# One inference step of a hybrid encoder: the same kernel with its SBUF tensors at other addresses

## The chip, the cores and the metric

The kernel runs on one core of a Trainium2 chip. The metric is the time of one execution on the device in microseconds (us), as the median of several runs. One of its executions was also taken with the profiler; the rows below come from it.

## What is computed

One layer for 1,024 prompt tokens and 8 x 16 sample tokens (1,152 tokens in all) of width 1,024, in float32:

```python
def layer_step(x, ...):
    hn = rms_norm(x, g_pre_mix)
    z, xbc, dt_raw, q, k, v = jnp.split(hn @ w_in, IN_SPLITS, axis=-1)      # 1024 -> 3080 columns
    ...                                    # group A: conv, SiLU, chunked state-space scan
    ...                                    # group B: rotary, differential attention over chunks
    mix = jnp.concatenate([y_ssd, y_att], axis=-1) @ w_out
    h = x + rms_norm(mix, g_post_mix)
    qx = (rms_norm(h, g_pre_x) @ wq_x).reshape(bsz, l, MEM_HEADS, MEM_HEAD_DIM)
    ...                                    # cross-attention, 4 heads of 256, 256 memory tokens
    h = h + rms_norm(ox @ wo_x, g_post_x)
    hn = rms_norm(h, g_pre_ffn)
    f = (jax.nn.silu(hn @ w_gate) * (hn @ w_up)) @ w_down                   # hidden width 2816
    h = h + rms_norm(f, g_post_ffn)
    return h, k, v, ssm_new, conv_new
```

The memory keys and values (256 tokens through wk_x and wv_x) are computed too.

## The kernel before

**Large products.** Each float32 operand is split in two float32r tensors, a high and a low half (names end in `_hi`/`_lo`, or in H/L). Helper `three` (L220 to L230) makes one product of three matmuls for each of 8 slices of the contraction: high x high (L225), high x low (L228), low x high (L229); in the trace the name in front is the operand that streams (moving), the one behind it is the one loaded into the array (stationary). A unit has 24 matmuls and fills one PSUM bank. There are three shapes: 256 columns stream (token-major products: the input projection, the two joins after `w_out` and `wo_x`, the memory products), 384 columns (the convolution part, `wq_x`, gate and up), and 512 columns (the down product of the feed-forward part).

**Weights.** All weights come as 130 items of [128, 1024] in order. SyncE loads an item into `w_raw` (2 buffers, L463), GpSimd makes `w_hi` (L522) and `w_lo` (L524) of it (4 buffers each), and TensorE gives a buffer back with the semaphore `w_used`.

**Stages, in order of time.** Norm and transposes of the tokens, and the input projection with the memory products between its units (to about 290 us); convolution part (to 390); the state-space scan (390 to 510); attention of the prompt and of the samples (510 to 780); join 1 and `wq_x` (780 to 1,000); cross-attention (1,000 to 1,140); join 2 (to 1,270); the feed-forward loop of 11 groups (to 2,085); the last norm, the sum and the stores.

**SBUF.** Tensors are given their places in the order in which they are declared, one behind the other, each start rounded up to 32 bytes. The first one of the kernel starts at byte 16,512 of a partition. Four large regions of 36,864 bytes each are shared over time by the tensors of an `overlay` call: the regions of H (also QL, KL, OL, the memory tensors), of NH (YT, MIX, QX, OH, Hback), of NL (V, E, H2, the hidden tensors, and others) and of XC (the staging tensors, KTt, QTt, YH, ACC). Behind them lies a fifth region of 16,640 bytes (gB0, xp, qkr, xs and others). All offsets inside these regions are fixed by the shapes; the token slices step by 512 bytes, a row of 1,152 tokens is 4,608 bytes, and a chunk of 384 tokens is 1,536 bytes, all multiples of 512.

Of the kernel before, what the change touches and what calls it, by code (L numbers as in the profile page):

```python
# [17 lines left out]
P = 128  # L18
# [42 lines left out]
S_N, S_Q, S_V, S_END = 0, 40, 76, 96  # L61
# [5 lines left out]
def build(nc, x_in, mem_in, wall, wdt, consts, vecs, gains, rows, kc, vc, h0, sconv, cmk, cmv,  # L67
          y_o, k_o, v_o, ssm_o, conv_o, mk_o, mv_o, zs_d, q_d, h_d):
    with ExitStack() as ctx:
        def sb(name, shape, dt=F32):  # L70
            return ctx.enter_context(nc.sbuf_tensor(name, shape, dt))
# [2 lines left out]
            return ctx.enter_context(nc.semaphore(name))  # L74


        raw = [sb(f"w_raw{i}", [P, WI]) for i in range(2)]
        whi = [sb(f"w_hi{i}", [P, WI], F32R) for i in range(4)]
        wlo = [sb(f"w_lo{i}", [P, WI], F32R) for i in range(4)]
        stat = sb("stat", [P, S_END])  # L80
        cst = sb("cst", [P, C_END])
        vec = sb("vec", [P, V_END])
        ones = sb("ones", [P, P])
# [2 lines left out]
        nlam = sb("nlam", [P, 1])  # L86
        lams = sb("lams", [P, 2])
        coef = sb("coef", [P, 1])
        cred = sb("cred", [P, 5])

# [1899 lines left out]
```

## Time and profile before

| | |
|---|---|
| median of 3 runs | 2127.1 us (2125.87 to 2129.05) |
| the profiled execution, its own time | 2123.53 us |
| its span, first to last instruction | 2121.3 us |
| mean granted TensorE clock | 0.948 of full speed |
| TensorE matmul busy | 1959.6 us, 92% |
| VectorE / ScalarE / GpSimd busy | 39% / 24% / 24% |
| mean DMA traffic | 76 GB/s |

Busy time of a matmul in the trace includes its way through the array, so neighbouring matmuls overlap; the pace of the engine is read from the distance of their starts. A "chain" is the sequence of work that ended last, followed back from the end.

### The profile page before, as it was taken

Reading aid. Unit: us, or ns where it says so; the run is one execution under the profiler, and the core shown is the slowest. Engines: PE = TensorE matmul, PEld = TensorE weight load, DVE = VectorE, ACT = ScalarE, POOL = GpSimd, SP = SyncE. Lnnn points to the kernel's source line nnn. Section 1 sums busy time; section 2 is a strip of 40 time slices with the busy share of each in tenths; the row PEclk is TensorE's granted clock in tenths of the full one; section 3 lists DMA queues with packets and bytes.
Section 4 is the critical chain, followed back from the end, with each engine's and each line's share of the span. In section 5 each row is a group of like instructions: output and inputs, shape, how many; then the busy total and the mean of one; then the engine's idle time right before and its main releaser. Section 6 shows DMA issues by size and latency. Waiting matters only on the chain.

```text
span 2121.3 us, 29729 instructions
## 1 busy us (share of the span) xinstructions
PE 1959.6 (92%) x12267; PEld 1828.7 (86%) x12267; DVE 830.8 (39%) x1618; ACT 514.0 (24%) x1248; POOL 511.3 (24%) x299
## 2 busy tenths in 40 slices
PE   7999999777789779898998989999999999999997
PEld 7999999766577679898897989998998898899895
DVE  4354026685667541700441171223223313322327
ACT  5200212473466441511331151100000010010002
POOL 3444352220000012321001232213223231331323
PEclk9999999996578889999998999999999999999998
DMA  5333231102200521221334122101101111110122
GB/s 205 113 115 119 88 124 40 57 26 86 99 1 1 183 110 41 90 99 64 136 120 169 41 91 78 41 21 60 40 27 53 40 40 40 40 59 20 59 109 99
DMA packets 55974, 161.25 MB, mean 76 GB/s; under 512 B 4160, under 2 KB 17984, under 8 KB 54464
## 3 DMA queue, kind: packets, MB, share of 16 engines
q1 hardware_dynamic: 33280, 115.04, 14.9%
q10 hardware_dynamic: 22592, 44.81, 6.1%
q8 instruction: 70, 1.15, 0.2%
q14 instruction: 32, 0.26, 0.0%
HBM read 131.67 MB, written 28.16 MB: 75 GB/s over the span
## 4 chain that ended last, share of the span: by engine, by line
PE 78%; DVE 11%; ACT 5%; issue 3%; DMA 2%; SPq 0%; ACTq 0%; DVEq 0%
PE bank L225 23%; PE bank L229 22%; PE bank L228 22%; DVE at_sm L1635 1%; PE bank L934 1%; PE bank L945 1%; PE bank L904 1%; DVE hid_l L1855 1%; PE bank L263 1%; DVE ACC L1864 1%; DVE ACC L1870 1%; DMA H<-scratch_h 1%; DVE H L326 1%; DVE E L1569 1%; PE bank L824 1%
## 5 line engine op out<-in xcount | busy, mean ns | idle before, releaser
L522 POOL CAST w_hi<-w_raw 128x1024 fp32r<-128x1024 f32 x130 | 140.9, 1084 | 1475.8 <-PE bank L225 1330.7
L225 PE MATMUL bank<-OH,w_hi 128*128 128x384 f32 x1056 | 355.1, 336 | 0.0
L229 PE MATMUL bank<-OH,w_lo 128*128 128x384 f32 x1056 | 354.8, 336 | 0.0
L228 PE MATMUL bank<-OL,w_hi 128*128 128x384 f32 x1056 | 354.8, 336 | 0.0
L524 POOL TENSOR_TENSOR w_lo<-w_raw,w_hi 128x1024 fp32r<-128x1024 f32 x130 | 323.0, 2485 | 10.4
L229 PE MATMUL bank<-w_hi,NL 128*128 128x256 f32 x864 | 241.1, 279 | 0.0
L1850 DVE TENSOR_TENSOR hr<-sg,bank 128x384 f32<-128x384 f32 x66 | 36.6, 554 | 438.0 <-PE bank L229 437.0
L225 PEld LDWEIGHTS bank<-OH,w_hi 128*128 128x128 f32 x1056 | 198.5, 188 | 0.4
L228 PEld LDWEIGHTS bank<-OL,w_hi 128*128 128x128 f32 x1056 | 198.5, 188 | 0.4
L229 PEld LDWEIGHTS bank<-OH,w_lo 128*128 128x128 f32 x1056 | 198.6, 188 | 0.0
L1864 DVE TENSOR_TENSOR ACC<-ACC,bank 128x512 f32<-128x512 f32 x180 | 122.2, 686 | 110.0 <-PE bank L229 110.0
L225 PE MATMUL bank<-w_hi,hid_h 128*128 128x512 f32 x396 | 157.5, 398 | 7.7 <-DVE ACC L1864 6.9
L229 PEld LDWEIGHTS bank<-w_hi,NL 128*128 128x128 f32 x864 | 164.3, 190 | 0.0
L225 PE MATMUL bank<-w_hi,NH 128*128 128x256 f32 x576 | 161.7, 281 | 0.0
L228 PE MATMUL bank<-w_lo,NH 128*128 128x256 f32 x576 | 160.7, 279 | 0.0
L228 PE MATMUL bank<-w_lo,hid_h 128*128 128x512 f32 x396 | 156.6, 396 | 0.0
L229 PE MATMUL bank<-w_hi,hid_l 128*128 128x512 f32 x396 | 156.6, 395 | 0.0
L1412 ACT ACTIVATE sg<-bank 128x384 f32<-128x384 f32 x66 | 32.5, 492 | 427.5 <-PE bank L229 427.5
L228 PE MATMUL bank<-NL,w_hi 128*128 128x384 f32 x384 | 129.0, 336 | 0.0
L228 PEld LDWEIGHTS bank<-w_lo,NH 128*128 128x128 f32 x576 | 109.3, 190 | 0.0
L225 PEld LDWEIGHTS bank<-w_hi,NH 128*128 128x128 f32 x576 | 109.1, 189 | 0.0
L1421 ACT ACTIVATE hid_h<-hr 128x384 fp32r<-128x384 f32 x66 | 34.7, 526 | 281.4 <-DVE hr L1850 281.4
(326 smaller groups left out, 3871.8 us busy)
## 6 DMA issues: line engine op xcount, KB each, us to landing
w_raw<-in_wall SPq DMA_DIRECT2D x130, 512.0 KB, 3.2
scratch_h<-H ACTq DMA_DIRECT2D x6, 1536.0 KB, 5.5
cK<-in_cmk SPq DMA_DIRECT2D x8, 1024.0 KB, 6.9
cV<-in_cmv SPq DMA_DIRECT2D x8, 1024.0 KB, 4.8
H<-in_x SPq DMA_DIRECT2D x1, 4608.0 KB, 14.8
H<-scratch_h SPq DMA_DIRECT2D x1, 4608.0 KB, 18.1
Hback<-scratch_h ACTq DMA_DIRECT2D x1, 4608.0 KB, 14.0
out_y<-Hback SPq DMA_DIRECT2D x9, 512.0 KB, 2.6
```

The source lines that it names most:

```text
L225: m = mm(out, ah, bh, start=(i == 0), stop=False)
L228: mm(out, ah, bl, start=False, stop=False)
L229: m = mm(out, al, bh, start=False, stop=(i == n - 1))
L263: m = nc.tensor.transpose(B[6 + j][:, tok(i)], src[:, tok(4 * j + i)], ident)
L326: STT(out=res[:, t, :], in0=mix[:, t, :], scalar=col(S_V, n), in1=res[:, t, :], op0=ALU.mult, op1=ALU.add).then_inc(j_res, 1)
L522: pool.tensor_copy(whi[s][:], raw[s % 2][:]).then_inc(w_hi, 1)
L524: pool.tensor_tensor(wlo[s][:], raw[s % 2][:], whi[s][:].bitcast(F32), ALU.subtract).then_inc(w_ready, 1)
L824: m = mm(B[sl][:, 0:PAST + DS], g("Qbd")[:, b, h, :], g(f"Kb{b}")[:, h, :], start=(h == 0), stop=(h == H - 1))
L1412: act_f(g(f"sg{n % 2}")[:], B[2 * (n % 3)][:, 0:NC], ACT.Silu).then_inc(f_sg, 1)
L1421: act_f(g(f"hid_h{gi % 2}{f}")[:, cs(c)], g(f"hr{n % 2}")[:], ACT.Copy).then_inc(f_hh, 1)
L1850: TT(g(f"hr{n % 2}")[:], g(f"sg{n % 2}")[:], B[2 * (n % 3) + 1][:, 0:NC], ALU.mult).then_inc(f_hr, 1)
L1864: TT(a, a, bank_[:, :], ALU.add).then_inc(f_de, 1)
```

## The change

Two declarations change, and no instruction.

```diff
+        stat = sb("stat", [P, S_END])
         raw = [sb(f"w_raw{i}", [P, WI]) for i in range(2)]
         whi = [sb(f"w_hi{i}", [P, WI], F32R) for i in range(4)]
         wlo = [sb(f"w_lo{i}", [P, WI], F32R) for i in range(4)]
-        stat = sb("stat", [P, S_END])
         cst = sb("cst", [P, C_END])
...
-        cred = sb("cred", [P, 5])
+        cred = sb("cred", [P, 5 + 80])
```

`stat` has 96 elements, 384 bytes, so the ten weight buffers (4,096 bytes each) move up by 384 bytes and `stat` moves down to the first place. `cst` and what follows it stay. `cred` grows from 20 to 340 bytes, of which 5 elements are used as before; with the rounding everything behind it moves up by 320 bytes.

| | first byte before | mod 512 | mod 2048 | first byte after | mod 512 | mod 2048 |
|---|---|---|---|---|---|---|
| w_raw0 (w_hi and w_lo follow in steps of 4,096) | 16,512 | 128 | 128 | 16,896 | 0 | 512 |
| cst | 57,856 | 0 | 512 | 57,856 | 0 | 512 |
| region of H | 63,168 | 192 | 1,728 | 63,488 | 0 | 0 |
| region of NH | 100,032 | 192 | 1,728 | 100,352 | 0 | 0 |
| region of NL | 136,896 | 192 | 1,728 | 137,216 | 0 | 0 |
| region of XC | 173,760 | 192 | 1,728 | 174,080 | 0 | 0 |
| fifth region | 210,624 | 192 | 1,728 | 210,944 | 0 | 0 |

## Rows read from the trace of the kernel before

**Rows 1.** The page: busy time by engine, and the chain's shares by engine.

```profile
PE 1959.6 (92%) x12267; PEld 1828.7 (86%) x12267; DVE 830.8 (39%) x1618; ACT 514.0 (24%) x1248; POOL 511.3 (24%) x299
...
PE 78%; DVE 11%; ACT 5%; issue 3%; DMA 2%; SPq 0%; ACTq 0%; DVEq 0%
```

**Rows 2.** Groups by shape on TensorE: moving, stationary operand, xcount, busy, mean ns.

```profile
L225 PE MATMUL bank<-OH,w_hi 128*128 128x384 f32 x1056 | 355.1, 336 | 0.0
...
L229 PE MATMUL bank<-w_hi,NL 128*128 128x256 f32 x864 | 241.1, 279 | 0.0
L225 PE MATMUL bank<-w_hi,NH 128*128 128x256 f32 x576 | 161.7, 281 | 0.0
...
L225 PE MATMUL bank<-w_hi,hid_h 128*128 128x512 f32 x396 | 157.5, 398 | 7.7 <-DVE ACC L1864 6.9 <-DVE ACC L1862 0.8
...
L228 PE MATMUL bank<-NL,w_hi 128*128 128x384 f32 x384 | 129.0, 336 | 0.0
...
L228 PE MATMUL bank<-w_lo,OH 128*128 128x256 f32 x288 | 82.0, 285 | 0.0
...
L225 PE MATMUL bank<-YH,w_hi 128*128 128x384 f32 x192 | 64.8, 337 | 0.0
...
L225 PE MATMUL bank<-mhi,w_hi 128*128 128x256 f32 x64 | 17.8, 279 | 0.0
```

**Rows 3.** Timeline of TensorE, 384 columns: start us, us; 12 matmuls further.

```profile
1499.82 0.34 PE L225 MATMUL bank<-OH,w_hi 128*128 128x384 f32 x1
...
1501.90 0.34 PE L225 MATMUL bank<-OH,w_hi 128*128 128x384 f32 x1
```

**Rows 4.** Timeline of TensorE, 512 columns; 26 matmuls further.

```profile
1383.88 0.40 PE L225 MATMUL bank<-w_hi,hid_h 128*128 128x512 f32 x1
...
1389.94 0.40 PE L229 MATMUL bank<-w_hi,hid_l 128*128 128x512 f32 x1
```

**Rows 5.** Timeline of TensorE, 256 columns of the weights stream; 23 matmuls further.

```profile
235.82 0.28 PE L225 MATMUL bank<-w_hi,NH 128*128 128x256 f32 x1
...
238.43 0.28 PE L229 MATMUL bank<-w_hi,mlo 128*128 128x256 f32 x1
```

**Rows 6.** The same with 256 columns of the memory tokens; 23 matmuls further.

```profile
95.13 0.28 PE L225 MATMUL bank<-mhi,w_hi 128*128 128x256 f32 x1
...
97.73 0.28 PE L229 MATMUL bank<-mhi,w_lo 128*128 128x256 f32 x1
```

**Rows 7.** 256 columns of the weights, earlier stretch; 21 matmuls further.

```profile
64.67 0.28 PE L225 MATMUL bank<-w_hi,NH 128*128 128x256 f32 x1
...
67.14 0.28 PE L225 MATMUL bank<-w_hi,NH 128*128 128x256 f32 x1
```

**Rows 8.** 384 columns against only 8 loaded columns; 13 matmuls further.

```profile
205.88 0.34 PE L225 MATMUL bank<-NH,wdh 128*8 128x384 f32 x1
...
208.13 0.33 PE L228 MATMUL bank<-NL,wdh 128*8 128x384 f32 x1
```

**Rows 9.** Plain float32 at full clock: 8 matmul passes of 272 columns.

```profile
753.54 2.00 PE L824 MATMUL bank<-Kb,Qbd 128*128 128x272 f32 x8
755.38 0.86 PE L847 MATMUL bank<-PTb,Vb 128*128 128x32 f32 x7
```

**Rows 10.** The chain in order of time, 16 columns streamed: start, us, what.

```profile
1044.81 3.48 PE bank L945 x32
```

**Rows 11.** The chain in order of time, its longest DMA pieces.

```profile
1.20 6.45 DMA H<-in_x
...
534.91 14.24 DMA V<-out_v
...
1140.65 18.08 DMA H<-scratch_h
```

**Rows 12.** Who waited for whom: us in total, times, longest.

```profile
POOL w_hi L522 <- PE bank L225: 1330.7, 95, 293.5
```

**Rows 13.** Windows of 50 us: busy, then granted clock, DMA share, GB/s.

```profile
550.00:600.00 50.00, 42.40 (x165) 32.86 (x165) 34.91 (x136) 27.68 (x85) 0.00 (x0) 0.60 0.00 1
```

## The prediction

> **What bounds the kernel now.** I read the page first. TensorE is busy 92% of the span, no other engine more than 39%, and 78% of the chain that ended last is TensorE's own work; DMA is on it with 2%, some 42 us [rows 1]. A layout can act only through the speed of reads and writes, so the question is whether any stream is slower than its engine. For that I read the groups by shape and then timelines of single units. The groups give the counts of the split products [rows 2]: 384 columns stream in 3 x 1056 + 384 + 4 x 192 + 3 x 24 = 4,392 matmuls (the OH row has two like it, the YH row three, and the products with 8 loaded columns are 3 groups of 24), 512 columns in 3 x 396 = 1,188, and 256 columns in 864 + 2 x 576 + 5 x 288 + 6 x 64 = 3,840.
>
> The timelines give the pace at a granted clock of 1.00. For 384 columns 12 matmuls take 1501.90 - 1499.82 = 2.08 us, 173.3 ns each [rows 3]; for 512 columns 6.06 us / 26 = 233.1 ns [rows 4]; for 256 columns 2.61 us / 23 = 113.5 ns [rows 5], which single starts put at 113.3. One column for each cycle of 2.4 GHz would be 160, 213.3 and 106.7 ns. So the stream is not at its engine's rate: it loses 6.7, 13.3 and 20 ns, that is 6.7 ns for each 512 bytes after the first. Over all these matmuls this is 3,840 x 6.7 + 4,392 x 13.3 + 1,188 x 20 = 108 us, 5% of the time, and it is the only place in which a layout could bring much. All these streams start 128 or 192 bytes behind a multiple of 512 now, and on one after the change.
>
> **The change, part by part.** No instruction, wait, DMA or byte moved is added or removed. `memset`s of `cred` write the same 5 elements. What can change is four prices.
>
> (a) *The moving stream of TensorE.* Is the loss a matter of address or of count? Nothing in the trace starts a float32r stream of 256 columns or more on a multiple of 512, so the answer is not there to be read; what is there speaks for count. First, the loss is (n - 1) x 6.7 ns for n blocks of 512 bytes, while a stream that starts off a multiple crosses n boundaries, not n - 1. Second, weights that start at 128 mod 512 and memory tokens that start at 192 have one pace, 113.5 and 2.60 us / 23 = 113.0 ns [rows 5, 6]: so boundaries of 128 bytes or less cost nothing, as the first stream lies on them and the second does not. Third, plain float32 takes (755.38 - 753.54) / 8 = 230 ns for a pass of 272 columns [rows 9], which is 2 cycles a column (226.7 ns) and 3 ns more, though these keys lie at every sort of offset (the heads step by 1,088 bytes) and each pass crosses 2 or 3 boundaries of 512: at half the rate the loss is gone. That looks like a feed which is a little too slow for a float at each cycle, with a first part that a buffer covers. I take 0 for this part; the bounds are a gain of all that address could explain, below, and 0.
>
> On the fixed part of a matmul the Trainium skill has a rule (TensorE: Matmul & The Clock Gate, "Wait — 56ns, not 53.3ns?"): warm, matmuls follow each other at N / 2.4 GHz plus about 2.5 ns. The rows of plain float32 agree; the float32r rows do not, with 13.3 ns at 384 columns and 20 at 512. By the Trainium skill's rule as it stands, with nothing else lost, 384, 512 and 256 columns would take 162.5, 215.8 and 109.2 ns, and if alignment gave that, the kernel would lose 4,392 x 10.8 + 1,188 x 17.3 + 3,840 x 4.1 ns = 84 us: about 2043 us. The Trainium skill has no figure by which an address would decide this.
>
> (b) *The weight load.* If loads and the stream met in the same part of the memory, a stream against 8 loaded columns would be faster than one against 128. It is not: 2.25 us / 13 = 173.1 ns [rows 8] against 173.3 [rows 3]. So no such meeting is paid for now; after the change both start at multiples of 512, a relation that has no row. I take 0.
>
> (c) *The two paces of 256 columns.* The input projection has stretches at 2.47 us / 21 = 117.6 ns [rows 7] with the same shapes, buffers and clock as the 113.5 ns stretches. By single starts 30 units, 720 matmuls, all before 170 us, run so. The pace changes only where a unit follows one of the memory units or at the start, and it holds for whole units: the order in which loads and streams interlock has two stable forms. The change could tip it in either direction: at best 720 x 4.3 ns = 3.1 us are gained, at worst the other 3,120 matmuls lose 4.3 ns each, 13.4 us. I take 0, since the tipping points are places in the order of work, which stays.
>
> (d) *Transfers.* The weight loads are far ahead: GpSimd waits 1330.7 us for TensorE to free a buffer [rows 12], so their speed is worth nothing. What shows are 42 us of DMA on the chain, 38.8 of them in three transfers into the regions of H and NL and the first token tile [rows 11]. A line of 4,096 bytes at 192 mod 512 touches 9 blocks of 512 bytes and an aligned one 8, so at most 1/9 of 42 us, 4.7 us, can be gained, and 0 at least; nothing in the change makes a transfer longer. With fixed latency in each of them I take 1 us.
>
> Here a rule speaks for the change: the Trainium skill (DMA: Bandwidth & Descriptors, "How a descriptor splits into AXI transactions") says that a transaction must start at a multiple of 256 bytes and that what lies before an unaligned start is fetched for nothing. For 4,096 bytes at 192 mod 256 that is 134 beats in place of 128, 4.5% of 42 us or 1.9 us if it holds for a destination as well; it stays inside the bounds given.
>
> (e) VectorE, ScalarE and GpSimd: their operands were multiples of 64 bytes and stay so. Were a TENSOR_TENSOR here 1% slower, the 11% of the chain that are VectorE's would cost 2.3 us. I take 0.
>
> **The sum.** The profiled execution took 2123.53 us with a span of 2121.3; 2123.5 - 1 = 2122.5. It was 3.6 us below the median of 2127.1, so against the median the forecast is 2126. The runs shown spread over 3.2 us, and a difference below 0.2% (4.3 us) can't be told from none.
>
> **The rivals.**
>
> *The loss goes by boundaries.* If each boundary of 512 bytes costs 6.7 ns with one of them covered, an aligned start crosses one less. Then 4,392 + 1,188 = 5,580 matmuls gain 6.7 ns, 37.2 us; the 3,840 of 256 columns can gain no more than down to the pace of the loads, 3.48 us / 32 = 108.8 ns [rows 10], 4.5 ns each or 17 us at most; with half of it 46 us, so 2081 us (2073 to 2090). For it speaks that all slow streams here are unaligned and that the loss comes in steps of just 512 bytes; against it the (n - 1) and [rows 9]. Boundaries of 256 bytes would give half, about 2105.
>
> *The two forms of the 256-column units tip.* All in the slow one: 2127.1 + 13.4 = 2140.5, slower. It decides from 1,000 matmuls (42 of the 160 units) that change over. For it speaks that weights and tokens, 64 bytes apart modulo 512 now, come to lie at equal offsets, and that the two forms exist; against it that the pace is the same wherever the moving operand lies [rows 5, 6]. If all tip to the fast form and the transfers gain their bound, 3.1 + 4.7 us, it would be 2119.
>
> *The clock.* Between 550 and 600 us the granted clock is 0.60 [rows 13], since TensorE waits often in the attention. Small shifts of a few ns there can move where the clock falls; 5 us of TensorE's work at 1.2 instead of 2.4 GHz cost 5 us. Either sign.
>
> **How the numbers follow.** No difference that can be told: 0.62. Boundaries of 512 or 256 bytes: 0.11. Small gain of the fast form with transfers: 0.07. All or much of the slow form: 0.11. The clock: 0.04 faster and 0.05 slower. So faster by over 0.2%: 0.22, same 0.62, slower 0.16. The likeliest case's own range is 2122 to 2131. The range for 8 in 10 reaches to 2114 and 2138: it takes in the small gain, the clock's cases and half of the slow form, and leaves out the boundaries' case and the full slow form, together under 0.2.
>
> **What would show it.** Right: starts 173.3, 233.1 and 113.5 ns apart as before, DMA on the chain within 5 us of 42, and a span within 4 us. Wrong at (a): 384 columns at 166.7 ns or below. Wrong at (c): the number of units with 117.6 ns is far from 30, or other units show a new pace. Wrong at (b): the 384-column pace rises while the products with 8 loaded columns keep theirs.

## The result, and the profile after

The changed kernel takes 2138.2 us in the median of 5 runs (2134.33 to 2140.89), the kernel before 2128.21 (2125.87 to 2134.62). The ratio is 1.0049 with a 95% interval of 1.003 to 1.0069: slower by half a percent, 10 us. The forecast was no difference, 2126 us. The profiled execution took 2137.9 us; its span grew from 2121.3 to 2135.7 us, by 14.4. That is more than the 10 us between the medians because the profiled execution of before (2123.53 us) was 4.7 us below its kernel's median, and that of after 0.3 below.

The page first, against [rows 1]:

```profile
PE 1970.3 (92%) x12267; PEld 1846.2 (86%) x12267; DVE 829.0 (39%) x1618; ACT 514.3 (24%) x1248; POOL 509.2 (24%) x299
...
PE 78%; DVE 12%; ACT 5%; issue 3%; DMA 2%; SPq 0%; ACTq 0%; DVEq 0%
```

VectorE, ScalarE and GpSimd do the same in the same time, and DMA keeps its 2%. TensorE's busy time grew by 10.7 us with the same count of matmuls. The groups by shape say where (TensorE, columns as in [rows 2]):

```profile
L225 PE MATMUL bank<-OH,w_hi 128*128 128x384 f32 x1056 | 353.1, 334 | 0.0
...
L229 PE MATMUL bank<-w_hi,NL 128*128 128x256 f32 x864 | 246.3, 285 | 0.0
L225 PE MATMUL bank<-w_hi,NH 128*128 128x256 f32 x576 | 164.5, 286 | 0.0
...
L225 PE MATMUL bank<-w_hi,hid_h 128*128 128x512 f32 x396 | 155.2, 392 | 8.3 <-DVE ACC L1864 7.4 <-DVE ACC L1862 0.8
```

The matmuls of 256 columns take longer (285 ns for 279), those of 512 columns less (392 for 398), and those of 384 nearly the same (334 for 336). As the busy times overlap, the timeline gives the paces. First the stretch that answers to [rows 7], then that of [rows 5]:

```profile
64.92 0.28 PE L225 MATMUL bank<-w_hi,NH 128*128 128x256 f32 x1
...
67.44 0.28 PE L225 MATMUL bank<-w_hi,NH 128*128 128x256 f32 x1
...
236.00 0.28 PE L225 MATMUL bank<-w_hi,NH 128*128 128x256 f32 x1
...
238.88 0.28 PE L225 MATMUL bank<-w_hi,mhi 128*128 128x256 f32 x1
```

The second row of each pair is 21 and 24 matmuls behind the first: 120.0 ns in both. The two paces of before, 117.6 and 113.5 ns, are gone, and a third has taken their place. For 384 and 512 columns (against [rows 3] and [rows 4]):

```profile
1499.71 0.33 PE L228 MATMUL bank<-OL,w_hi 128*128 128x384 f32 x1
...
1502.83 0.33 PE L228 MATMUL bank<-OL,w_hi 128*128 128x384 f32 x1
```

```profile
1397.80 0.39 PE L228 MATMUL bank<-w_lo,hid_h 128*128 128x512 f32 x1
...
1404.82 0.39 PE L229 MATMUL bank<-w_hi,hid_l 128*128 128x512 f32 x1
```

3.12 us / 18 = 173.3 ns, as before; 7.02 us / 31 = 226.5 ns, 6.6 less than the 233.1 of [rows 4].

The means over all starts of a width in the split products, left out those that waited, account for the whole growth of the span:

| | 256 columns, x3840 | 384 columns, x4392 | 512 columns, x1188 | sum |
|---|---|---|---|---|
| before, ns | 114.32 | 173.35 | 233.26 | |
| after, ns | 119.98 | 173.41 | 227.26 | |
| difference x count, us | +21.7 | +0.3 | -7.1 | +14.9, span +14.4 |

The transfers have no weight in this sum. The chain in order of time has the same reload as [rows 11] with 17.40 us instead of 18.08, but the first tile with 6.99 instead of 6.45:

```profile
1.20 6.99 DMA H<-in_x
...
1156.96 17.40 DMA H<-scratch_h
```

### The profile page after: what moved, and what is told of

It is laid out like the page before. It is cut to its first block, busy times and chain, and to the rows that moved or that the text cites. A ratio compares the mean times of both kernels' runs of the same rounds, so it can differ in the third digit from the quotient of the medians.

```text
span 2135.7 us, 29729 instructions
## 1 busy us (share of the span) xinstructions
PE 1970.3 (92%) x12267; PEld 1846.2 (86%) x12267; DVE 829.0 (39%) x1618; ACT 514.3 (24%) x1248; POOL 509.2 (24%) x299
## 4 chain that ended last, share of the span: by engine, by line
PE 78%; DVE 12%; ACT 5%; issue 3%; DMA 2%; SPq 0%; ACTq 0%; DVEq 0%
PE bank L225 23%; PE bank L229 22%; PE bank L228 22%; DVE at_sm L1635 2%; PE bank L934 2%; PE bank L945 1%; PE bank L904 1%; DVE hid_l L1855 1%; PE bank L263 1%; DVE ACC L1864 1%; DVE ACC L1870 1%; DMA H<-scratch_h 1%; DVE H L326 1%; DVE E L1569 1%; DVE MT L1576 1%
## 5 line engine op out<-in xcount | busy, mean ns | idle before, releaser
L229 PE MATMUL bank<-w_hi,NL 128*128 128x256 f32 x864 | 246.3, 285 | 0.0
```

Source lines behind the costliest of these rows:

```text
L229: m = mm(out, al, bh, start=False, stop=(i == n - 1))
```

## The experiments

Below, r is the start of the region minus the start of the weights. It is 64 bytes modulo 256 before and 0 after. All paces in tables are means of start-to-start distances in the trace. The programs of matmuls alone (m1, m2, m3) ran once each, at a granted clock of 1.00 throughout. Two theories stood: that each operand's own start counts (A), and that the relation of the streamed and the loaded operand counts (R).

**m1_sweep.** A program of matmuls alone, 156 cases of 48:

```python
for j, (n, m, s) in enumerate(configs()):
    mm(bank[2][:, 0:16], sta[:, 0:P], mov[:, 0:16], start=True, stop=True)
    for i in range(48):
        mm(bank[j % 2][:, 0:n], sta[:, s // 4:s // 4 + P], mov[:, m // 4:m // 4 + n],
           start=(i == 0), stop=(i == 47))
```

> Only matmuls on TensorE: 156 cases of 48 equal float32r matmuls with 128 loaded columns (256, 384 or 512 streamed), separated by one of 16 columns; nothing of the layer is computed. What varies is the start of the streamed and of the loaded operand modulo 512 bytes (and a few of the loaded one modulo 2048). Theory R (relation: the stream and the load of the next matmul meet in the memory): the pace depends only on the difference of the two starts; equal shifts of both change nothing; difference 0 gives 120 ns at 256 columns and 227 at 512 as in the changed kernel, a difference of 64 gives 113.3 or 117.7. Theory A (each operand's own start): with the loaded operand fixed, a stream at 0 mod 512 gives 120 ns and one at 128 or 192 gives 113.3, and moving the loaded operand alone changes nothing. My recorded view (count of blocks, no address) would give one pace for each width.

Its timeline, with the separators of 16 columns between the cases; streamed from 0, loaded from 0, 32 and 64 bytes; then 512 columns, loaded from 0, 32 and 64:

```profile
97.20 5.99 PE L126 MATMUL bank<-mov,sta 128*128 128x256 f32 x48
103.03 0.17 PE L124 MATMUL bank<-mov,sta 128*128 128x16 f32 x1
103.06 5.92 PE L126 MATMUL bank<-mov,sta 128*128 128x256 f32 x48
...
108.85 5.70 PE L126 MATMUL bank<-mov,sta 128*128 128x256 f32 x48
...
836.37 11.13 PE L126 MATMUL bank<-mov,sta 128*128 128x512 f32 x48
...
847.37 11.44 PE L126 MATMUL bank<-mov,sta 128*128 128x512 f32 x48
...
858.67 11.45 PE L126 MATMUL bank<-mov,sta 128*128 128x512 f32 x48
```

The first three rows of 48 differ in the start of the loaded operand (and in the output bank, which alternates from case to case; the first and the third have the same one), and their time goes from 5.99 to 5.70 us; at 512 columns the order is the other way round. The settled pace, from 32 starts in the middle of each case that streams from 0, by the loaded start minus the streamed one:

| difference, bytes | 0 | 32 | 64 | 96 | 128 | 160 | 192 | 224 |
|---|---|---|---|---|---|---|---|---|
| 256 columns, ns | 120.0 | 118.3 | 113.3 | 117.4 | 118.7 | 120.1 | 117.8 | 117.8 |
| 384 columns, ns | 173.3 | 173.3 | 173.3 | 173.4 | 175.9 | 176.7 | 173.3 | 173.3 |
| 512 columns, ns | 226.7 | 233.3 | 233.3 | 234.4 | 232.1 | 233.4 | 229.0 | 233.3 |

From 256 to 480 bytes the row repeats within 0.2 ns, and 512, 1024 and 1536 give the value of 0 within 0.3. Both starts shifted together by 64 to 448 bytes at difference 0 give 119.9 to 120.0, 173.3 and 226.7 to 227.0 ns. At difference 64, the same joint shifts give 113.3 to 113.4 ns six times and 117.8 twice at 256 columns. So theory A falls: the relation counts, modulo 256 bytes. The changed kernel's three paces are just the column of difference 0.

The relation alone does not fix the pace at every difference, though. At 256 columns m1 has 117.8 ns three times at difference 192 and 113.3 twice, both with the stream at 64 bytes modulo 256, and 116.7 beside 117.8 at 224. At 384 columns and difference 64 it has 173.3 ns six times, 174.6 or 174.7 seven times and 176.7 once. At difference 0, and at 512 columns, all cases of a difference agree within 0.4 ns.

**e1_weights_only, e2_regions_only, e3_both_384.** The two halves of the change alone, and both operands moved with r kept:

```diff
+        stat = sb("stat", [P, S_END])        # e1: only this, r = 192
         raw = [sb(f"w_raw{i}", [P, WI]) for i in range(2)]
...
-        stat = sb("stat", [P, S_END])
...
-        cred = sb("cred", [P, 5])
+        cred = sb("cred", [P, 5 + 80])       # e2: only this, r = 128
+        cred = sb("cred", [P, 5 + 96])       # e3: this and the move of stat, r = 64
```

> Only stat is moved: weights at 0 mod 512, regions stay at 192. Theory A: the 256- and 512-column streams are the weights' own, so all of the effect is here: 120.0 ns and 227 ns, about 2138 us. Theory R: the difference of the starts is now 192 (before 64, after 0), so the paces are others than in both kernels; 2138 us only by accident, and the 384-column pace may move too.

> Only cred grows: regions at multiples of 2048, weights stay at 128 mod 512. Theory A: 256 and 512 columns keep 113.3/117.7 and 233.3 ns, about 2128 us, and only the 384-column pace could move. Theory R: the difference is now 384, a third set of paces.

> Weights at 0 mod 512 as after, regions at 64 mod 512 (cred 16 elements more), so the difference of 64 bytes of the kernel before is kept. Theory R: the paces of the kernel before, 113.3 with some units at 117.7, 233.3, and about 2128 us. Theory A: 120.0 and 227 ns, about 2138 us.

**e4_before_hidden_0, e5_after_hidden_64.** The hidden tensors are the operand loaded against the 512-column streams, and no other product uses them, so they can be moved for themselves. e4 is the kernel before with them at difference 0; e5 is the changed kernel with them at 64, and its regions 256 bytes lower (`cred` with 5 + 16), so at 256 modulo 512:

```diff
-                         [(f"hid_{a}{g}{f}", [P, NTOK], F32R) for g in range(2) for f in range(2) for a in "hl"],
-                         [("under_jk", [P, 4 * NTOK], F32), ("jk", [P, D], F32)]))
+                         [("under_hid", [P, 48], F32)] +      # e5: 16
+                         [(f"hid_{a}{g}{f}", [P, NTOK], F32R) for g in range(2) for f in range(2) for a in "hl"] +
+                         [("over_hid", [P, 16], F32)],        # e5: 48
+                         [("under_jk", [P, 4 * NTOK + 64], F32), ("jk", [P, D], F32)]))
```

> The kernel before with only the hidden tensors moved by 192 bytes inside their region (difference to the weights 0 instead of 64 modulo 256; the regions behind move by 256, which is no change modulo 256). Theory R modulo 256: the 1,188 matmuls of 512 columns go from 233.3 to 227 ns, 7.5 us less, ratio 0.9965; 256 and 384 columns as before. If only the regions' starts modulo 512 or 2048, or the weights' own starts, mattered: no change in the 512-column pace.

> The changed kernel with the regions 256 bytes lower (0 modulo 256 still, no longer at multiples of 2048) and the hidden tensors 64 bytes up. Theory R modulo 256: 256 columns stay at 120 ns, 384 at 173.3, 512 columns go back to 233.3 ns, so 7.5 us above the changed kernel, about 2146 us, ratio 1.0085 to before. If multiples of 2048 mattered, the 256-column pace would leave 120 ns.

All five, with the differences of the paces to the kernel before times the counts 3,840, 4,392 and 1,188:

| | r | 256 ns | 384 ns | 512 ns | sum us | span us | median us | ratio (95%) |
|---|---|---|---|---|---|---|---|---|
| before | 64 | 114.32 | 173.35 | 233.26 | | 2121.3 | 2126.59 with e1 to e3, 2125.6 with e4, e5 | |
| e1 | 192 | 117.54 | 175.01 | 229.05 | +14.7 | +15.1 | 2140.56 | 1.0059 (1.0037 to 1.0081) |
| e2 | 128 | 119.00 | 175.87 | 232.83 | +28.5 | +28.1 | 2151.23 | 1.0104 (1.0078 to 1.013) |
| e3 | 64 | 113.93 | 173.34 | 233.31 | -1.5 | -0.8 | 2124.4 | 0.9987 (0.9969 to 1.0005) |
| e4 | 64, hidden 0 | 115.05 | 173.34 | 226.99 | -4.7 | +1.8 | 2119.16 | 0.9966 (0.9953 to 0.9979) |
| e5 | 0, hidden 64 | 119.97 | 173.39 | 233.31 | +21.9 | +20.1 | 2143.8 | 1.0082 (1.0066 to 1.0098) |

e3 settles it in the real kernel: its weights start at multiples of 512 just as in the changed kernel, and it has the paces and the time of the kernel before. The timeline of e3 at the place of [rows 5], 23 matmuls apart, reads as there, 113.5 ns:

```profile
235.73 0.28 PE L225 MATMUL bank<-w_hi,NH 128*128 128x256 f32 x1
...
238.34 0.28 PE L229 MATMUL bank<-w_hi,mlo 128*128 128x256 f32 x1
```

e2 alone (+28.1 us of span) costs more than the whole change (+14.4). By its time alone e1 would have spoken for theory A, which expected about 2138 us where 2140.56 were measured; its paces do not, 117.5 and 229.1 ns where A wanted 120.0 and 227. In e1 and e2 the 256- and 512-column paces are within 1 ns of m1's table at 192 and 128 bytes. The 384-column products stream the region and load the weights, so their difference is -r: 64 bytes in e1 (measured 175.0, where m1 has 173.3 to 176.7) and 128 in e2 (175.9 in both).

e4 and e5 have the 512-column paces that were written down for them, and e5 the other two as well. In e4's down product 24 starts from 1387.19 to 1392.63 us give 226.7 ns:

```profile
1387.19 0.39 PE L227 MATMUL bank<-w_hi,hid_h 128*128 128x512 f32 x1
...
1392.63 0.39 PE L227 MATMUL bank<-w_hi,hid_h 128*128 128x512 f32 x1
```

The profiled execution of e4 was the longest of its seven (2125.29 us), so its span does not show what the median and the ratio do. Its trace says where the gain went. From the first to the last matmul of 512 columns it took 6.5 us less than the kernel before, but join 2 took 4.4 us more. Of these some 2.7 are 26 of its 36 units at 117.8 ns, where none ran so before (26 x 24 matmuls x 4.4 ns); the granted clock at its start was lower too, 0.74 for 0.78 over 21 us. In all, 55 of the 160 units of 256 columns ran in this slower form, against 30 before and 16 in e3, all three with the same difference of 64. So "256 columns as before" did not hold in this execution, and how many units are slow is no property of the layout alone. By its median e4 is faster than both kernels. In e5 the regions of H, NH and NL are no longer at multiples of 2048, nor of 512, and 256 columns still take 120 ns. (The regions behind NL are, as the padding of the hidden tensors moves them up by 256 bytes again.)

**m2_fine.** The same program in steps of 8 bytes, with other loads, widths and separators:

> Only matmuls again, nothing of the layer: finer steps of 8 bytes of the difference over 256 bytes, loads of 8, 32, 64 and 96 columns, widths from 128 to 480, and for the differences 64 and 192 separators of different width. Theory R (load and stream meet): with 8 loaded columns the pace doesn't depend on the difference, and the dependence grows with the loaded columns; the lowest paces over all differences are 113.3, 173.3 and 226.7 ns, so no start gives one column per cycle. A rival, that the stream alone sets the loss by its own reads: the paces with 8 loaded columns show the same dependence on the difference. If the two forms at 256 columns are an interlock, which of 113.3 and 117.8 ns appears at 64 depends on the separator in front.

The lowest paces over 32 differences are 113.3, 173.3 and 226.7 ns: no start gave one column per cycle. From 128 to 224 columns the pace was 111.7 ns (once 111.8) at each of the three differences tried, whatever the width. That looks like the load of 128 columns as the longer part, which no shorter load at these widths tested. With 8 loaded columns the pace at 256 columns was 116.7 ns at difference 0 and 113.3 elsewhere, at 512 columns 226.6 at 0 and 231.7 elsewhere; at 384 it was 174.7 at 0 and 173.3 elsewhere. So the dependence does not vanish with a short load, against what was expected; at 256 columns it shrinks (116.7 instead of 120.0). Nor does it grow steadily with the loaded columns: at difference 128, 256 columns took 113.3, 120.0, 116.7, 120.0 and 118.8 ns with 8, 32, 64, 96 and 128 of them. And at difference 64, 256 columns ran at 113.3 behind five of nine separators and at 117.8 behind the four others; at 192 all nine gave 117.8. The width of the separator is not what decides, though: behind 16 columns the same case ran at 113.3 ns early in m2 and at 117.8 here.

**m3_own_or_next.** Even and odd matmuls with different starts:

> Only matmuls, nothing of the layer. Even and odd matmuls stream from and load from different starts, so that the difference between a stream and its own loaded operand and the one between a stream and the operand loaded for the next matmul can be set apart. If a stream meets the load of the next matmul, the paces follow the next difference (0: 120 ns at 256 columns and 227 at 512; 64: 113.3 or 117.8 and 233.3) whatever the own one is; if the own pair counts, they follow the own difference. A second part repeats 256 columns behind nine separators at the differences 0, 64, 88, 168 and 192: the interlock view expects one pace of 120.0 at 0, two paces at 64, and at 88 and 168 either 113.3 throughout or two again.

This one did not tell. With the own difference 0 and the next ones 64 and 192, 256 columns took 116.7 ns, and with the next difference 0 and the own ones 64 and 192 they took 116.7 too; only when both were 0 was it 120.0. At 512 columns both cases gave 231.7, and 226.7 to 226.8 with both at 0. Neither pair alone sets the pace. The second part gave 119.8 to 120.1 at difference 0 behind all nine separators, 113.3 and 117.8 at 64 again, 113.3, 116.7 and 120.0 at 88, and 113.3 and 120.0 at 168. But at 64 the separators of 16 and 48 columns gave 113.3 here and 117.8 in m2, and that of 32 the reverse. Two cases of the first part that follow each other show it best: the same separator of 16 columns, the same addresses (difference 64), and only the output bank and the case ahead of them differ. Their paces are 113.3 and 117.8 ns:

```profile
142.74 5.71 PE L121 MATMUL bank<-mov,sta 128*128 128x256 f32 x48
...
148.32 5.90 PE L121 MATMUL bank<-mov,sta 128*128 128x256 f32 x48
```

## Why the prediction was wrong

**The step that failed** is (b): "after the change both start at multiples of 512, a relation that has no row. I take 0." The relation was named, and its price set at nothing because a stream against 8 loaded columns ran like one against 128, 173.1 and 173.3 ns. That comparison was made at 384 columns, the width that reacts least: in m1 it moves by 3.4 ns over all differences, and between the 192 bytes of the kernel before and 0 not at all, while 256 columns move by 6.7 and 512 by 7.7. Nor did it hold the relation fixed: the slices with 8 loaded columns step by 32 bytes in a region that moves with the streamed one, so their rows mix all differences in steps of 32, before and after alike. For the same reason the sign given for (b), the 384-column pace rising against theirs, could not appear. In its place the runs showed a term of +14.9 us: the relation cost 21.7 us at 256 columns (120.0 ns for 114.3) and gave back 7.1 at 512 (227.3 for 233.3).

**(a), the stream's own start.** The view that the loss goes not by boundaries of 512 bytes was right: joint shifts at difference 0 change nothing, and the 384-column stream keeps 173.3 ns with one boundary less. That it goes by count and by no address, one pace for each width, was wrong. The argument from [rows 5, 6] was too short. Weights and memory tokens were 64 bytes apart one way or the other, and m1 has 113.3 ns at both 64 and 192, so equal paces did not show that place is free. The loss in steps of 6.7 ns is not a fixed tax either: at 512 columns it is 13.3 ns at difference 0 and 20 at 64.

The Trainium skill (SBUF — State Buffer, "Who interferes with whom") gives TensorE two independent read ports, one for the moving operand and one for LDWEIGHTS, and says that it never waits on anyone. If that were all, the loaded operand's start could not change the pace. In m1 it does, from 113.3 to 120.1 ns at 256 columns, and the measurement decides.

**(c), the two paces of the 256-column units.** That there are two stable forms is borne out: m2 and m3 have both at the same addresses, by what ran before. That a tipping was to be taken as 0, "since the tipping points are places in the order of work", missed that the relation decides which forms exist; at difference 0 every case with 128 loaded columns ran at about 120 ns. At an equal relation the places do vary, with 30, 16 and 55 slow units in before, e3 and e4. The rival, all in the slow form at 2140.5 us, came close in time for a reason that was not quite its own: not 117.6 ns for all, but a third pace of 120.0 ns, and a gain at 512 columns that it did not have.

**(d) and (e), transfers and the other engines.** The bound of 4.7 us is not contradicted: the large reload gained 0.7 us and the first tile lost 0.5, one execution each. Over all seven profiles the reload tells more. It took 17.27 to 17.56 us where H starts at a multiple of 256 bytes (after, e2, e5) and 17.80 to 18.08 where it does not (before, e1, e3, e4), some 3%, in the direction that the prediction gave for such starts. The 42 us of DMA on the chain was read off the rounded 2%: its pieces add up to 48.4 us before and 41.1 after, and 14.24 of them before, the V reload, are off the chain after. VectorE's busy time went from 830.8 to 829.0 us. **The boundaries' rival** fell with m1 and e3. **The clock** played no part that shows: 0.948 and 0.951 in the mean.

What stays open is what meets inside. The pace depends on the difference of the two starts modulo 256 bytes, on the width and on what ran before, for short loads too, and m3 could not say whether the own or the next load takes part. A collision in the memory was argued, not shown.

## What to carry to other kernels

Where TensorE streams float32r at full clock and loads for every matmul, the distance of the two operands modulo 256 bytes is a price of its own, 6% of a 256-column matmul between 64 and 0 bytes here, and each product has its own best one: difference 0 is among the slowest for 256 columns and the fastest for 512. Where two forms exist, a difference promises only a set of paces. Read start-to-start paces, not busy times, and tabulate them by difference in one short program before an address is moved. Then move single tensors, as e4 does, instead of whole regions, and pad in steps that leave the other relations alone.

## What was not expected of the hardware

- The pace of float32r matmuls with a load each depends on the difference of the two starts with a period of 256 bytes, though not on it alone: 113.3 to 121.9 ns at 256 columns in steps of 8 bytes, 173.3 to 180.0 at 384, 226.7 to 234.4 at 512.
- The same instructions at the same addresses keep 113.3 or 117.8 ns for whole runs of 48, by what ran before them.
- From 128 to 224 streamed columns the pace was 111.7 ns (once 111.8) at the differences 0, 64 and 192, with 128 loaded.
- A reload of 4.6 MB into SBUF took some 3% less time in the three layouts in which its destination starts at a multiple of 256 bytes than in the four in which it does not.
